# A two-block transformer on one core: 96 half tiles in the two-part matmul form, a causal head loop, and moved read-outs

## The reference

```python
logit_own = jnp.where(dist_own >= 0, logit_own, -jnp.inf)   # first block: causal
x = x + y @ w_out[l]                                        # second block: wa2, wb2
x = x + memory_attention(h, rmsnorm(mem, mem_norm[l]), w_xq[l], w_xk[l], w_xv[l], w_xo[l])
```

## Time and profile before

| | us |
|---|---|
| median of 3 runs | 2697.28 |
| the profiled execution, its own time | 2699.36 |
| its span, first to last instruction | 2697.3 |
| TensorE busy (PE) | 2647.7 |
| GpSimd busy (POOL) | 2201.5 |
| ScalarE busy (ACT) | 1254.1 |
| VectorE busy (DVE) | 1148.9 |

### The profile page before, as it was taken

One profiled execution on the slowest core, in us unless ns is written; L12 is line 12 of the kernel. 1 busy time (PEld: TensorE's weight loads), 2 busy tenths in 40 slices (PEclk: granted clock), 3 DMA queues, 4 the chain that ended last, 5 costly groups with the idle time before them and its releaser, 6 DMA issues.

```text
span 2697.3 us, 43085 instructions
## 1 busy us (share of the span) xinstructions
PE 2647.7 (98%) x16754; PEld 2393.7 (89%) x16754; DVE 1148.9 (43%) x1340; ACT 1254.1 (46%) x1496; POOL 2201.5 (82%) x889
## 2 busy tenths in 40 slices
PE   8999999998999999999999999999999999999998
PEld 8979998897888888888899888999998888888886
DVE  5677757675555554423354245711211111113233
ACT  5445444545444444444654444533544444444444
POOL 7878865786998988899898755867878888889997
PEclk9999999999999999999999999999999999999999
DMA  9998976664565655455455533534455555555553
GB/s 375 377 398 321 395 300 246 247 253 163 208 259 215 253 218 209 171 201 195 173 188 195 187 143 115 219 141 157 172 189 188 189 189 189 189 189 189 189 200 125
DMA packets 101765, 588.02 MB, mean 218 GB/s; under 512 B 11240, under 2 KB 13416, under 8 KB 45200
## 3 DMA queue, kind: packets, MB, share of 16 engines
q1 hardware_dynamic: 93600, 570.07, 56.8%
q10 hardware_dynamic: 8048, 16.26, 1.7%
HBM read 579.98 MB, written 8.40 MB: 218 GB/s over the span
## 4 chain that ended last, share of the span: by engine, by line
PE 74%; POOL 14%; issue 9%; DVE 2%; ACT 0%; POOLq 0%; DMA 0%; DVEq 0%; ACTq 0%; SPq 0%
PE ps L1275 28%; PE ps L1280 15%; POOL w_lo L523 14%; PE ps L1241 6%; PE ps L1248 6%; PE ps L1243 6%; PE ps L1298 3%; PE ps L1300 3%; PE ps L1306 3%; PE ps L1879 1%; PE ps L1854 1%; PE ps L1562 0%; PE ps L1369 0%; PE ps L1532 0%; PE ps L1531 0%
## 5 line engine op out<-in xcount | busy, mean ns | idle before, releaser
L523 POOL TENSOR_TENSOR w_lo<-raw,w_hi 128x1024 fp32r<-128x1024 f32 x884 | 2201.1, 2505 | 477.9 <-ACT w_hi L546 474.7
L546 ACT CAST w_hi<-raw 128x1024 fp32r<-128x1024 f32 x884 | 923.7, 1051 | 1135.9 <-PE ps L1280 571.3
L1275 PE MATMUL ps<-a_both,w_hi 128*128 128x512 f32 x3328 | 833.4, 392 | 0.0
L1275 PEld LDWEIGHTS ps<-a_both,w_hi 128*128 128x128 f32 x3328 | 598.5, 189 | 107.1
L1241 PE MATMUL ps<-a_both,w_hi 128*128 128x256 f32 x2384 | 597.9, 288 | 7.3 <-issue 2.9
L1243 PE MATMUL ps<-a_both,w_hi 128*128 128x256 f32 x2384 | 587.8, 284 | 0.0
L1280 PEld LDWEIGHTS ps<-a_both,w_lo 128*128 128x128 f32 x3328 | 453.7, 190 | 33.1 <-POOL w_lo L523 0.8
L1241 PEld LDWEIGHTS ps<-a_both,w_hi 128*128 128x128 f32 x2384 | 459.8, 193 | 12.6 <-issue 5.7
L1280 PE MATMUL ps<-a_both,w_lo 128*128 128x256 f32 x3328 | 464.3, 282 | 0.0
L1243 PEld LDWEIGHTS ps<-a_both,w_hi 128*128 128x128 f32 x2384 | 460.1, 193 | 0.7
L1248 PE MATMUL ps<-a_both,w_lo 128*128 128x256 f32 x2384 | 335.7, 283 | 0.0
(11 more groups left out here) (243 smaller groups left out, 1623.3 us busy)
## 6 DMA issues: line engine op xcount, KB each, us to landing
raw<-stream SPq DMA_DIRECT2D x440, 1024.0 KB, 4.8
arena<-ada SPq DMA_DIRECT2D x185, 512.0 KB, 6.4
work<-ada SPq DMA_DIRECT2D x7, 512.0 KB, 7.2
arena<-memT SPq DMA_DIRECT2D x4, 512.0 KB, 9.9
res<-xT SPq DMA_DIRECT2D x4, 512.0 KB, 12.7
v_spill<-arena ACTq DMA_DIRECT2D x4, 512.0 KB, 3.4
k_spill<-arena ACTq DMA_DIRECT2D x4, 512.0 KB, 7.3
rel_rows<-rel_row ACTq DMA_DIRECT2D x4, 512.0 KB
```

Source lines behind the costliest of these rows:

```text
L523: pool.tensor_tensor(w_lo[:, h % SLOTS], raw_half(h), w_hi[:, h % SLOTS].bitcast(F32), ALU.subtract).then_inc(lo_ready, 1)
L546: act.copy(w_hi[:, base % 4], raw[:, tile_slot, (base % 2) * HALF:(base % 2 + 1) * HALF]).then_inc(hi_ready, 1)
L1275: pe.matmul(acc_two(g + turned)[:, f], w_hi[:, h % SLOTS, cols(k, f)], a_both[:, c0 + k], start=first and k == 0, stop=False, skip_group_c ...
```

## The change

1. Halves of 256 output columns by 4 chunks of inputs in the two-part form (half_pair), for win2 groups 2 to 5, groups 2 and 3 of wa2 and wb2, and groups 1 to 3 of xq and xo. Each old group of 512 columns becomes two pair groups of 256 with numbers of their own. The weights of these groups are laid out for it on the host (_in_pairs). Groups before those in WHOLE stay in the old form.
2. Their read-outs: pair_rows (three operations) and pair_residual (two or four). VectorE does mix_out of wb2 group 1 ahead of the low part and sum of lnmem quarter 0, and pair read-outs ahead of sums. ScalarE's conditions for overwriting a_hi name later halves.
3. The first block's heads (u < 8) leave out keys 128 to 255 for queries 0 to 127, in the bias loads, scores, exponentials, transposes, copies and value products.
4. Two points go from ROW_POINTS; ada_sum(3) moves from behind state_out(10) to just before state_out(11).
5. The read-out of kn_r's first four chunks moves from side(12), behind back(15), to before back(15).

```diff
-          ("wc", 2), ("wq", 1), ("krot", 1), ("wk", 5), ("uq", 3), ("rot", 1), ("ukv", 4), ("wa2", 4),
-          ("wb2", 4), ("xq", 4), ("xo", 4), ("gu", 22), ("down2", 2)]
+          ("wc", 2), ("wq", 2), ("krot", 1), ("wk", 8), ("uq", 3), ("rot", 1), ("ukv", 4), ("wa2", 6),
+          ("wb2", 6), ("xq", 7), ("xo", 7), ("gu", 22), ("down2", 2)]
+def win2_pair(g, s):
+    return G0["wq"] + s if g == 2 else G0["wk"] + 2 * (g - 3) + s
+WHOLE = {"wa2": 2, "wb2": 2, "xq": 1, "xo": 1}
+def pair_group(name, g, s):
+    return G0[name] + WHOLE[name] + 2 * (g - WHOLE[name]) + s
-ROW_POINTS = [... (105, 112), (111, 112), (129, 128), (130, 128),
+ROW_POINTS = [... (105, 112), (111, 112), 
               (138, 140), ...
+        def acc_pair(G):
+            return ps[:, 2 * (G % 2):2 * (G % 2) + 2, :].rearrange("p f (a t) -> p f a t", a=2)
+        def seen(u, qt):
+            return P if u < 8 and qt == 0 else S
+        def keys(u, qt):
+            return slice((qt + 1) * S - seen(u, qt), (qt + 1) * S)
...
-                act.wait_ge(half_used, hx + 26 + 2 * q)
+                act.wait_ge(half_used, hx + 29 + q)
...
-            his(ho + 26, 4)
-            operand("lnffn", 0, 0, ho + 26)
-            his(ho + 30, 2)
-            operand("lnffn", 1, 4, ho + 28)
+            his(ho + 26, 6)
+            operand("lnffn", 0, 0, ho + 29)
+            his(hg, 1)
+            operand("lnffn", 1, 4, ho + 30)
             ffn_gain(2)
-            his(hg, 2)
-            operand("lnffn", 2, 8, ho + 30)
+            his(hg + 1, 1)
+            operand("lnffn", 2, 8, ho + 31)
+            def half_pair(h, G, c0, first, last):
+                def cols(k, f):
+                    return slice(k * 256 + f * P, k * 256 + (f + 1) * P)
+                wait_high(h)
+                for k in range(4):
+                    for f in range(2):
+                        pe.matmul(acc_pair(G)[:, f], w_hi[:, h % SLOTS, cols(k, f)], a_both[:, c0 + k],
+                                  start=first and k == 0, stop=False, skip_group_check=True)
+                wait_half(h)
+                for k in range(4):
+                    for f in range(2):
+                        mm = pe.matmul(acc_pair(G)[:, f, 0, :], w_lo[:, h % SLOTS, cols(k, f)], a_hi[:, c0 + k, :],
+                                       start=False, stop=last and k == 3, skip_group_check=True)
+                mm.then_inc(half_used, 1)
+            def in_pairs(name, n, per, at=0):
+                g, s = n // per, n % per * 2 // per
+                G, h, step = pair_group(name, g, s), H0[name] + n, n % (per // 2)
+                if step == 0:
+                    pe.wait_ge(evac[G % 2], G // 2)
+                half_pair(h, G, at + 4 * step, step == 0, step == per // 2 - 1)
...
-                state_out(h)
-                if h == 10:
+                if h == 11:
                     pe.wait_ge(y_done, 5)
                     ada_sum(3, 4, S)
+                state_out(h)
...
+                    for kt, qt in ((0, 0), (0, 1), (1, 1)):
+                        at = keys(u, qt).start + kt * P
+                        mm = pe.transpose(ps[:, 6 + u % 2, (kt + qt) * P:(kt + qt + 1) * P], prob[:, u % 2, at:at + P],
+                                          ident)
...
+            def pair_rows(dst, G, row, halves):
+                dve.wait_ge(half_used, halves)
+                hi, lo = acc_pair(G)[:, :, 0, :], acc_pair(G)[:, :, 1, :]
+                link(dve.tensor_tensor(dst, hi, over_chunks(row, 2), ALU.mult))
+                link(dve.tensor_tensor(lo, lo, over_chunks(row, 2), ALU.mult))
+                settle()
+                dve.tensor_tensor(dst, lo, dst, ALU.add).then_inc(evac[G % 2], 1)
+            def pair_residual(q, s, G, halves, row=None):
+                dve.wait_ge(half_used, halves)
+                hi, lo = acc_pair(G)[:, :, 0, :], acc_pair(G)[:, :, 1, :]
+                r = res[:, 4 * q + 2 * s:4 * q + 2 * s + 2, :]
+                if row is not None:
+                    link(dve.tensor_tensor(hi, hi, over_chunks(row, 2), ALU.mult))
+                    link(dve.tensor_tensor(lo, lo, over_chunks(row, 2), ALU.mult))
+                    settle()
+                link(dve.tensor_tensor(r, hi, r, ALU.add))
+                settle()
+                dve.tensor_tensor(r, lo, r, ALU.add).then_inc(evac[G % 2], 1)
+                dve.wait_ge(evac[G % 2], G // 2 + 1)
...
-                if i == 12:
-                    out_rows(kn_r[:, 0:4, :], G0["ukv"], row_c, hk2 + 1)
...
-                if i == 26:
-                    mix_out("wa2", 2, row_a)
-                if i == 30:
-                    mix_out("wa2", 3, row_a)
+                if i in (24, 26, 28, 30):
+                    j = (24, 26, 28, 30).index(i)
+                    mix_pair("wa2", 2 + j // 2, j % 2, row_a)
...
+                    if u == 14:
+                        out_rows(kn_r[:, 0:4, :], G0["ukv"], row_c, hk2 + 1)
                     back(u + 1)
...
             mix_out("wb2", 0, row_b)
+            mix_out("wb2", 1, row_b)
             low_of_ring("lnmem", 0, 0)
             add_up(K0["lnmem"], part(0))
-            mix_out("wb2", 1, row_b)
+            mix_pair("wb2", 2, 0, row_b)
             low_of_ring("lnmem", 1, 4)
+            mix_pair("wb2", 2, 1, row_b)
             add_up(K0["lnmem"] + 1, part(1))
-            mix_out("wb2", 2, row_b)
-            mix_out("wb2", 3, row_b)
+            mix_pair("wb2", 3, 0, row_b)
+            mix_pair("wb2", 3, 1, row_b)
```

More of the change, by code:

```diff
@@ L835, in wait @@
                     else:
-                        G = G0[name] + q
-                        act.wait_ge(evac[G % 2], G // 2 + 1)
+                        pair = name in WHOLE and q >= WHOLE[name]
+                        for G in [pair_group(name, q, s) for s in range(2)] if pair else [G0[name] + q]:
+                            act.wait_ge(evac[G % 2], G // 2 + 1)
                 return wait
@@ L1094, in _ @@
                 his(h0 + 5, 1)
+                his(h0 + 6, 2)
+                copies_x(u)
                 if x == 2:
@@ L1524, in scores @@
                 for qt in range(2):
-                    o = ps[:, 4 + u % 2, qt * S:(qt + 1) * S]
+                    o = ps[:, 4 + u % 2, keys(u, qt)]
                     a = slice(qt * P, (qt + 1) * P)
                     if u < 16:
-                        mm = pe.matmul(o, q_r[:, h, a], k_r[:, h, :], start=True, stop=True, skip_group_check=True)
+                        mm = pe.matmul(o, q_r[:, h, a], k_r[:, h, 0:seen(u, qt)], start=True, stop=True,
+                                       skip_group_check=True)
                     else:
@@ L1561, in values @@
                 for kt in range(2):
-                    mm = pe.matmul(o, v[:, kt, h * P:(h + 1) * P], probT[:, u % 2, kt * S:(kt + 1) * S],
+                    n = P if u < 8 and kt else S
+                    mm = pe.matmul(o[:, S - n:S], v[:, kt, h * P:(h + 1) * P], probT[:, u % 2, kt * S:kt * S + n],
                                    start=kt == 0, stop=kt == 1, skip_group_check=True)
@@ L1727, in win2_half @@
                 g, s = n // 8, n % 8
-                G, h = win2_group(g), H0["win2"] + n
+                h = H0["win2"] + n
+                if 2 <= g < 6:
+                    G = win2_pair(g, s // 4)
+                    if s % 4 == 0:
+                        pe.wait_ge(evac[G % 2], G // 2)
+                    half_pair(h, G, (4 * s + 8) % 16, s % 4 == 0, s % 4 == 3)
+                    return
+                G = win2_group(g)
                 if s == 0:
@@ L1811, in mix_half @@
                 half_T(h, acc(G), c0 + 2 * s, s == 0, s == 3)
-            G = win2_group(5)
-            pe.wait_ge(evac[G % 2], G // 2 + 1)
+            for s in range(2):
+                G = win2_pair(5, s)
+                pe.wait_ge(evac[G % 2], G // 2 + 1)
             pe.wait_ge(tok_ready, 3)
@@ L2082, in front @@
                 neg = small[:, 4 * (u % 2):4 * (u % 2) + 2]
+                lo = keys(u, 0).start
                 if u < 16:
@@ L2608, in _, with win2_out @@
             parts_ready(21)
-            out_rows(q_r[:, 0:4, :], win2_group(2), row_a, hw2 + 24)
+            def win2_out(dst, g):
+                for s in range(2):
+                    pair_rows(dst[:, 2 * s:2 * s + 2, :], win2_pair(g, s), row_a, hw2 + 8 * g + 4 * s + 4)
+            win2_out(q_r[:, 0:4, :], 2)
             def rotated(n, G, chunks):
@@ L2652, in mix_out, with mix_pair @@
                 residual_row(g, acc(G), H0[name] + 4 * g + 4, evac[G % 2], G // 2 + 1, row)
+            def mix_pair(name, g, s, row):
+                pair_residual(g, s, pair_group(name, g, s), H0[name] + 4 * g + 2 * s + 2, row)
             def side(i):
@@ L2892, with _in_pairs @@
 DOWN_ORDER = [0, 2, 1, 3] + list(range(4, 44))
+def _in_pairs(w, first=0, last=None):
+    w = [w[:, 512 * g:512 * g + 512] for g in range(w.shape[1] // 512)]
+    last = len(w) if last is None else last
```

(1 more changed line is left out.)

88 lines of the change are left out of this document (57 added, 31 removed).

## The result

The changed kernel takes **2682.36 us**, the median of 5 runs (2680.90 to 2684.92), against 2697.28 for the kernel before: a ratio of 0.9946, 95% interval 0.9935 to 0.9958. The forecast was 2681.3. Its profiled execution has a span of 2680.5 us, 16.8 less than before; the total agrees with the forecast better than the terms do, as the stages show.

A forecast was written before the change was run, and what follows sets the result against it. TensorE's own queue, busy 98% of the span, was taken as the bound. Terms -8.35 - 2.5 - 5.2 - 1.2 + 0.8 + 0.5 = -15.95 us gave 2681.3 us from a median of 2697.28; 8 in 10 range 2676.5 to 2688.5.

The forecast's parts named there:

- Parts 1 and 2: 96 halves in two-part form, 0.087 us less each, 8.35 us less; their read-outs add waits of 0.8 and 0.5 us.
- rival C: A 512-column matmul alternating between two banks takes 0.240 us, so pair halves gain 0: 2689.6 us; chance 0.08.
- Krot's wait: At the key rotation, wk0 waits for wq1's banks; with a read-out of 2.0 us the 0.89 us wait grows by 0.8.
- rival A: Stalls move more than they go: 4 us wait at state_out(13), slow clock there and behind krot: 2687.0 us; chance 0.20.
- In wb2: Group (3,0) needs (2,0) read out; VectorE has 11.3 us of work against 11.2: 0.5 us of new wait, bounds 0 and 2.
- (3,1): The next wb2 group after (3,0): about 0.2 us left over by the same sum, so no wait.
- D: Rival: small groups' read-outs late at all 28 places, 0.8 us each, slower than before: 2702.4 us; chance 0.03.
- Part 3: First block's causal heads: 0.33 us less for each of eight, 2.5 us less in all, bounds 1.5 and 2.6.
- Part 4: Ada rows and ada_sum(3): both stalls go, about 1.9 us of wait returns at state_out(13); 5.2 us less, bounds 2 and 7.5.
- Part 5: kn_r's first read-out before back(15) fills VectorE's idle time: 1.2 us less, bounds 0.8 and 1.9.
- everything behind it ends 1.15 us earlier: VectorE operations behind kn_r's moved first read-out at back(15) all end 1.15 us earlier.
- its own list of signs: Wrong if pair halves lie 2.88 apart, pair read-out waits appear at over three places, or the clock falls where it held.

The follow-up runs named there:

- e11: The kernel before, unchanged, run and profiled again: 2695.65 us, ratio 1.0000.
- e7: The changed kernel with the two points back in ROW_POINTS, ada_sum(3) left before state_out(11): 2683.80 us, ratio 0.9950 to the kernel before.
- e8: The changed kernel with ada_sum(3) back behind state_out(10), the two points still gone: 2681.80 us, ratio 0.9938 to the kernel before.
- e2: The changed kernel with the first eight heads again computed over the full 256 by 256: 2686.64 us.
- e6: The changed kernel with the second read-out of kn_r made twice, one more VectorE operation ahead of the rotation's: 2683.32 us in a single execution.
- e3: The changed kernel with the two points back in ROW_POINTS and ada_sum(3) back behind state_out(10): 2688.81 us, ratio 0.9975 to the kernel before.
- e4: Pair halves with their read-outs alone, the change's other three parts undone: 2690.75 us, ratio 0.9981 to the kernel before.
- e10: The changed kernel run again, unaltered: 2682.68 us, ratio 0.9948 to the kernel before.

## Why the prediction came out as it did
**Parts 1 and 2: right.** 96 halves brought 0.082 to 0.087 us each, 8.0 us by the stages (6.6 net and 1.4 of waits) against 8.35; rival C falls, since the wide matmul on two banks takes 0.230. Krot's wait grew from 0.89 to 1.68 us (0.8 forecast), and the clock held, so that half of rival A falls too. In wb2 0.7 us came where 0.5 was forecast, 0.6 of it before (3,1) and 0.1 before (3,0), for which it was forecast: I had given (3,1) 0.2 us to spare with a low part of 2.80 us, and it took 3.48. No other pair read-out is late, so D falls.

**Part 3: the mechanism right, the size not.** 3.9 us, outside my bounds of 1.5 to 2.6. The term "four value matmuls of 256 columns take 0.86" took four records for four matmuls. They are two float32 matmuls of two records each; halving one saves 0.216, not 0.108, and so in the scores. Per head 0.21 + 0.10 + 0.21 = 0.53, eight heads 4.2, less 0.3 of wait at the first.

**Part 4: right in sum, 6.2 against 5.2.** Both stalls and both slow stretches went, and the wait came back at state_out(13), 1.2 us against 1.9:
```profile
428.74 0.26 PE L1411 MATMUL ps<-folded,con 128*32 128x16 f32 x8
...
442.59 0.65 PE L1544 MATMUL ps<-work,stage_v 128*64 128x256 f32 x2 [1.25 <-DVE work L2423]
```
Against e11 in place of the first profile it is 4.7. That the move of ada_sum(3) earns anything was wrong: by itself it would have ended the stalls too, for a longer wait and a slow stretch at state_out(13) (e7), but beside the points it costs 1.3 us (e8).

**Part 5: wrong, and the step that failed is** "everything behind it ends 1.15 us earlier". I took VectorE's operations between SBUF tensors as pieces of fixed length; the earlier trace rows did not show what stood beside them. The sum ended 0.3 us earlier. The move put L2736 into the course of a GpSimd half: a wait of 2.6 at L1583 against 1.7 + 0.94 before, a gain of 0.3 at most (e2), and in six of seven executions a slow stretch that costs 1.5 to 4.5 us. Two waits of 1.7 and 0.9 left the clock alone; one of 2.6 did so once. The prediction gave the longer wait behind L1531 no price for the clock, and by its own list of signs it is wrong here: the clock falls at a place where it held.

**The total was right partly by luck**: parts 3 and 4 brought 2.4 us more than forecast, part 5 4.0 less, the pair halves 0.5 less, and 3.1 us of the spans' difference arose before 350 us, where the instructions are the same. Without them the stages make 13.7 us, and 12.2 against e11 in place of the first profile; the medians say 14.9, interval 11.3 to 17.5.

## What to carry to other kernels
Before an operation of VectorE between two SBUF tensors is moved, look at GpSimd's timeline at the new place: its length is decided there, and here a start 1.13 us earlier became an end 0.3 us earlier. Count matmuls in the code and records in the trace before a record's time is given to a matmul. And compare two profiles stage by stage, with one repeat of each, before a difference is credited to the change: here 3 us of 17 arose where both kernels have the same instructions.

## What was not expected of the hardware
**VectorE and GpSimd exclude each other when VectorE reads two SBUF tensors.** In the trace of the kernel before, 119 operations of VectorE on 1024 elements with both inputs in SBUF began in the course of a GpSimd low part. All ended 1.08 to 1.09 us after it, whenever they had begun (in the changed kernel 111 of 114 did), and took 1.36 to 3.45 us. 38 that began with GpSimd idle took 1.21 to 1.29, and 162 with an operand in PSUM that began in the course of a low part took 1.20 to 1.29. GpSimd waits in turn: 3.33 us in the changed kernel's fence for a half that takes 2.37 in e6's. The Trainium skill ("SBUF — State Buffer", section "SBUF: two separate sides") calls this an exclusive lock on a shared port pair, which whoever starts first holds for a whole instruction, VectorE's operations with two SBUF inputs included; every one of these rows agrees with it. It also accounts for why an ada row took 1270, 2249 or 3439 ns in the earlier trace rows: not variation, but phase.

**The same wait, with and without a slow clock.** Behind the 1.79 us at ada_sum(3) the granted clock fell in e3 and in the first profile, and held in e4 and e11 (windows around it, first e3, then e11; the number before the last two is the clock):
```profile
420.00:434.00 14.00, 12.21 (x88) 11.16 (x86) 7.11 (x10) 5.06 (x9) 4.86 (x3) 0.88 0.44 169
```
```profile
418.00:432.00 14.00, 12.21 (x99) 11.13 (x98) 8.49 (x12) 6.21 (x10) 6.36 (x3) 1.00 0.52 199
```
It was so behind the 2.6 us at L1583 too: 1.00 over 18 us in e2, 0.72 in e10. What decides it stays open. From 350 us on, nearly all other stages repeat within 0.1 us from execution to execution; so a forecast has to carry the clock behind a short wait as a chance, here of 1.5 to 4.5 us.
